# A two-layer decoder step: 32x32 tiles for the delta rule's inverse, three halving sums in the layer norm, a first weight tile loaded a phase ahead, and another order of the merged loop

## The chip, the cores and the metric

The kernel runs on one core of a Trainium2 chip, in one launch. The metric is device microseconds of the whole program, the median of several runs. One further execution was recorded by the profiler; the rows below are of that execution. TensorE is called PE (its weight loads PEld), VectorE DVE, ScalarE ACT, GpSimd POOL, and SyncE, which issues most transfers, SP. Each engine runs its own instructions in order and waits on counting semaphores.

## The reference

The program is one step of a decoder of two layers (model width 1024) for a prompt of 1024 rows and 8 sample rows together (1032 columns in the kernel's transposed layout). Cut to what matters:

```python
def even_mixer(x, ...):                    # layer 0
    qkv_a, beta_a, a_a, gate_a, q_b, kv_b, g_b = split_cols(x @ w_in, EVEN_SIZES)
    o_a, S_new = gated_delta_chunked(qa, ka, va, g, beta, S0)    # 4 heads of 128
    o_b, rows, new_buf = nsa_mixer(q_b, kv_b, gates, hist, ...)  # 8 query heads of 64, 2 groups
    return concat(rms_norm(o_a) * silu(gate_a), o_b) @ w_out

def gated_delta_chunked(...):              # for every chunk and head
    A  = where(strict, (k * beta) @ k.T * Ldec, 0)
    Tm = triangular_solve(eye + A, eye)    # the inverse, by levels in the kernel
    u, w = Tm @ (v * beta), Tm @ (k * beta * exp(gam))
    v_new = u - w @ S;  o = qg @ S + qk @ v_new;  S = S * glast + kd.T @ v_new

# nsa_mixer: three softmax branches with gates: compressed blocks of 32 rows, selected blocks of 64, window of 512
# layer 1: gated linear attention (GLA) in chunks of 16, then @ w_out
# after every mixer and every SwiGLU: x = layer_norm(ALPHA * x + f(x))
def swiglu(x, wg, wu, wd): return (silu(x @ wg) * (x @ wu)) @ wd
```

## The kernel before, in words

Matrices with weights are computed with three matmuls each (high*high, low*high, high*low parts; lines L565 to L567), with x transposed: 8 blocks of 128 features by 1032 columns, handled as NB = 3 groups of CW = 344 columns. Phases follow each other with a barrier between them: the even projection (0 to 341 us), small gates, **the merged loop** (`even_core_phase`, 377 to 1234), the sample rows of the even mixer (`sample_even_phase`, to 1337), **the chain of layer 0** (`chain_phase`: output projection, norm, SwiGLU, norm, next projection; to 2521), GLA (`gla_phase`, to 2733), and **the chain of layer 1** (to the end).

**The merged loop** interleaves three things on every engine in an order written by hand. The 1024 prompt rows are 8 tiles; `Fori i` runs 4 times, each time two chunks c (halves), each with 8 units u. A unit is one (row tile t, KV group g) of the sparse attention: `scores_win` (L1560, L1562: window and compressed scores), its maximum on DVE (`max_win`, L1925 to L1931), its exponentials on ACT (`exp_win`, L1771 to L1773), its weights on DVE (`weigh_win`, L1946 to L1950, called done by the semaphore `win_scaled`), `turn_win` (L1584: transposes of the weights on PE, in groups 0 and 1 of up to four blocks), ACT's copies of them (`keep_win`, L1784), and products with the values (`values_sel`, `values_win`); likewise `scores_sel` (L1549, always for the next unit j+1), `max_sel`, `exp_sel` (L1763), `weigh_sel`, `turn_sel` (L1572), `keep_sel`. Besides these a chunk has 24 steps `delta(c, k)` of the delta rule, three to a unit (k = 3u, 3u+1, 3u+2), and one page of the cache per unit (`pages_mean`, `pages_turn`, `pages_kept`, `pages_score`). In a chunk with many keys (t = 4 to 7) the local weights have two groups, in the others one or two.

The delta rule's inverse is built by 7 levels, `lv = (k - 3) // 2`. Before, every level works on tiles of 4 heads of 128x128: POOL masks A with a table (`masked`, L1507), PE multiplies it with D (`each`, L1639, four 128x128x128 matmuls), ACT copies the product (L1828), PE multiplies again twice, DVE subtracts from D and DT (L2008, L2010). k = 4 to 12 are the levels 0 to 4, k = 13 to 16 the levels 5 and 6. k = 3 makes A = KK and QK, two `each`, after waiting for ACT's copies VB and KE (L1820, L1823).

**The chain**: its first tile of the output projection (n = 0) waits for POOL's split of the weights into parts (`split`: L509 cast, L511 subtraction) and for h_lo (L940, DVE, 8 pieces). A norm goes by column group c: `total` (L897 additions), a matmul for the mean (L582), `centre` (L907), squares on ACT (L796), `fold` (L902: sum of 8 squares blocks by one `tensor_reduce`), a matmul for the variance, scale, low. At the end of layer 1 `turn(n)` turns each of 9 row tiles by 8 transposes (L709) and makes its row mean by 8 matmuls of one column (L715); DVE then scales the rows (L1071, L1078) for the output.

Of the kernel before, what the change touches and what calls it, by code (L numbers as in the profile page):

```python
# [47 lines left out]
LEVELS = 7  # L48


def constants():
# [4 lines left out]
    for lv in range(LEVELS):  # L56
        s = 1 << lv
        row, col = i[None, :], i[:, None]
        level[:, lv] = (row // (2 * s) == col // (2 * s)) & (row // s % 2 == 1) & (col // s % 2 == 0)
    upper = (i[:, None] <= i[None, :]).astype(np.float32)  # L60
# [8 lines left out]
    for h in range(HEADS):  # L69
# [8 lines left out]
        "c_ident": ident, "c_level": level.reshape(P, -1), "c_upper": upper, "c_causal": causal, "c_oldest": oldest,  # L78
# [289 lines left out]
class Norm:  # L368
# [3 lines left out]
    def __init__(self, nc, tag, ln, rows, low):  # L372
        self.ln, self.rows, self.low = ln, rows, low
        (self.totalled, self.mean_ready, self.centred, self.squared, self.folded, self.var_ready, self.logged,
         self.rstd_ready, self.scaled, self.rounded, self.low_ready) = [nc.alloc_semaphore(tag + s) for s in (
            "_totalled", "_mean_ready", "_centred", "_squared", "_folded", "_var_ready", "_logged", "_rstd_ready",
            "_scaled", "_rounded", "_low_ready")]


def chain_phase(nc, r, layer, tag, lay, load_out, reload, odd=None):  # L380
# [23 lines left out]
    with phase(nc) as ctx:  # L404
# [7 lines left out]
        o_hi = at("o_w_hi", [P, 3, KD, P], F32R, lay["o_hi"])  # L412
        F, Flo = at("f", [P, KF, N], F32, 0), at("f_lo", [P, KF, N], F32R, 0)
# [8 lines left out]
        sums_b = at("sums_b", [P, NB, CW], F32, KD)  # L422
        flat_f, flat_h1 = [t[:].rearrange("p k n -> p (k n)") for t in (F, H1)]
# [26 lines left out]
        def _(sp):  # L450
            def fetch_out(n):
                if n >= 3:
                    sp.wait_ge(product_o, 3 * (n - 2))
                for dst, src in load_out(n):
                    sp.dma_start(o_raw[:, n % 3][dst], src).then_inc(w_in_o[n % 3], 16)
# [26 lines left out]
            for n in range(3):  # L482
# [5 lines left out]
            for n in range(3, KD):  # L488
# [17 lines left out]
        def _(pool):  # L506
# [6 lines left out]
            def split_out(n):  # L513
                s = n % 3
                split(w_in_o[s], 16 * len(load_out(n)) * (n // 3 + 1), w_split_o, n, o_hi[:, s], o_raw[:, s], o_lo[:, s])
# [24 lines left out]
            for n in range(3):  # L540
# [3 lines left out]
            for n in range(3, KD):  # L544
# [7 lines left out]
            for n in range(2 * KD):  # L552
                split_down(n)
                if odd and n >= 13:
                    collect(evicted_d, 3 * KD, sums_b, summed_b, n - 12)
            if odd:
                for m in range(4, 6):
                    collect(evicted_d, 3 * KD, sums_b, summed_b, m)
# [2535 lines left out]
```

## Time and profile before

| | us |
|---|---|
| median of 3 runs (lowest, highest) | 3650.86 (3647.32, 3657.77) |
| the profiled execution | 3649.13 |
| its span | 3647.3 |
| PE busy in the span | 3336.8 (91%) |
| DVE busy | 1271.2 (35%) |
| POOL busy | 1016.9 (28%) |
| ACT busy | 699.8 (19%) |

The profiled execution is 1.8 us longer than its span and 1.7 us under the median. PE is busy nearly all the time in the projections and the two chains; in the merged loop, the sample rows and GLA it is not.

### The profile page before, as it was taken

How to read it: one execution, taken by the hardware profiler on the slowest of the kernel's cores; microseconds unless marked ns; L12 is line 12 of the kernel's file. 1: busy time of each engine (PE TensorE's matmuls, PEld its weight loads, DVE VectorE, ACT ScalarE, POOL GpSimd, SP SyncE). 2: the span in 40 equal slices, each digit the busy share in tenths (PEclk: the TensorE clock that was granted, in tenths of full speed). 3: DMA queues.
4: the chain of work that ended last, by engine and by line, in shares of the span. 5: the costliest groups of instructions: out<-in, count | busy, mean ns of one | idle time of the engine just before them, and what ended most of it. 6: DMA issues, size and time to landing. Idle time of an engine off the chain costs nothing. (4 is left out here: it accounts for less than half of the span.)

```text
span 3647.3 us, 55768 instructions
## 1 busy us (share of the span) xinstructions
PE 3336.8 (91%) x22086; PEld 3032.4 (83%) x22086; DVE 1271.2 (35%) x2434; ACT 699.8 (19%) x1424; POOL 1016.9 (28%) x619
## 2 busy tenths in 40 slices
PE   8998768898989769999999999998889899999998
PEld 7998546565656559999999999997659899999998
DVE  6712535555555533300004216112553500003123
ACT  1101334443444321200001102001320300001011
POOL 3542111211122024233333242331336133333220
PEclk9999889899988779999999999998779999999999
DMA  4122332323233560111111112111113011111111
GB/s 131 46 46 56 109 111 82 91 81 94 81 89 85 173 232 24 41 46 46 46 46 46 48 41 81 47 46 30 47 43 115 24 46 46 46 46 47 48 48 67
DMA packets 327512, 247.87 MB, mean 68 GB/s; under 512 B 28368, under 2 KB 322009, under 8 KB 325644
## 3 DMA queue, kind: packets, MB, share of 16 engines
q1 hardware_dynamic: 325956, 234.57, 21.8%
q10 hardware_dynamic: 720, 8.55, 0.6%
q8 instruction: 127, 2.08, 0.2%
q0 software_dynamic: 640, 2.10, 0.2%
q14 instruction: 69, 0.57, 0.1%
HBM read 220.59 MB, written 45.63 MB: 73 GB/s over the span
## 5 line engine op out<-in xcount | busy, mean ns | idle before, releaser
L565 PE MATMUL ps<-X_rounded,c_w_hi 128*128 128x344 f32 x2712 | 872.7, 322 | 6.0 <-DVE c_xla L921 5.4
L567 PE MATMUL ps<-X_rounded,c_w_rounded 128*128 128x344 f32 x2712 | 868.3, 320 | 0.0
L566 PE MATMUL ps<-c_xla,c_w_hi 128*128 128x344 f32 x2112 | 674.5, 319 | 0.0
L509 POOL CAST c_w_hi<-c_w 128x1024 fp32r<-128x1024 f32 (+1 forms) x145 | 165.4, 1141 | 1283.8 <-DMA c_w<-in_w_ffn_gate 710.2
L565 PEld LDWEIGHTS ps<-X_rounded,c_w_hi 128*128 128x128 f32 x2712 | 509.6, 188 | 8.7 <-issue 6.6
L567 PEld LDWEIGHTS ps<-X_rounded,c_w_rounded 128*128 128x128 f32 x2712 | 509.3, 188 | 0.0
L566 PEld LDWEIGHTS ps<-c_xla,c_w_hi 128*128 128x128 f32 x2112 | 398.1, 189 | 0.7 <-issue 0.2
L511 POOL TENSOR_TENSOR c_w_rounded<-c_w,c_w_hi 128x1024 fp32r<-128x1024 f32 (+1 forms) x145 | 387.1, 2670 | 11.6
L565 PE MATMUL ps<-c_f_hi,c_w_hi 128*128 128x344 f32 x1056 | 342.9, 325 | 12.6 <-DVE c_f_lo L987 12.4
L567 PE MATMUL ps<-c_f_hi,c_w_rounded 128*128 128x344 f32 x1056 | 340.8, 323 | 0.0
L566 PE MATMUL ps<-c_f_lo,c_w_hi 128*128 128x344 f32 x1056 | 339.1, 321 | 0.0
L983 DVE TENSOR_TENSOR c_f<-c_silu,ps 128x344 f32 x108 | 55.4, 513 | 763.0 <-PE ps L567 763.0
L929 DVE SCALAR_TENSOR_TENSOR X<-X,ps 128x344 f32<-128x344 f32 x144 | 72.7, 512 | 488.2 <-PE ps L567 488.2
L565 PEld LDWEIGHTS ps<-c_f_hi,c_w_hi 128*128 128x128 f32 x1056 | 200.5, 190 | 16.1 <-DVE c_f_lo L987 15.8
L295 PE MATMUL ps<-X_rounded,in_even_w_hi 128*128 128x344 f32 (+1 forms) x648 | 209.1, 323 | 4.7 <-DVEq L324 2.7
L297 PE MATMUL ps<-X_rounded,in_even_w_rounded 128*128 128x344 f32 (+1 forms) x648 | 208.3, 321 | 0.0
L296 PE MATMUL ps<-Xl_in_even,in_even_w_hi 128*128 128x344 f32 (+1 forms) x648 | 207.7, 321 | 0.0
L566 PEld LDWEIGHTS ps<-c_f_lo,c_w_hi 128*128 128x128 f32 x1056 | 200.8, 190 | 0.4 <-issue 0.2
L567 PEld LDWEIGHTS ps<-c_f_hi,c_w_rounded 128*128 128x128 f32 x1056 | 200.2, 190 | 0.0
L838 ACT ACTIVATE c_silu<-ps 128x344 f32<-128x344 f32 x108 | 49.4, 457 | 768.6 <-PE ps L567 768.6
L566 PE MATMUL ps<-c_xlb,c_w_hi 128*128 128x344 f32 x600 | 191.7, 320 | 0.0
L565 PE MATMUL ps<-c_h_hi,c_o_w_hi 128*128 128x344 f32 x384 | 128.2, 334 | 23.6 <-POOL c_o_w_lo L511 23.6
(501 smaller groups left out, 5468.6 us busy)
## 6 DMA issues: line engine op xcount, KB each, us to landing
X<-in_cache_nsa_kv SPq DMA_DIRECT2D x256, 192.0 KB, 2.4
c_w<-in_w_ffn_gate SPq DMA_DIRECT2D x44, 512.0 KB, 3.8
c_w<-in_w_ffn_up SPq DMA_DIRECT2D x44, 512.0 KB, 3.8
c_w<-in_w_ffn_down SPq DMA_DIRECT2D x32, 704.0 KB, 4.7
v_packed<-in_cache_nsa_kv SPq DMA_DIRECT2D x256, 64.0 KB, 2.5
in_even_w<-in_w_in_even SPq DMA_DIRECT2D x52, 256.0 KB, 3.1
c_w<-in_w_in_odd SPq DMA_DIRECT2D x50, 256.0 KB, 3.3
x_spilled<-H ACTq DMA_DIRECT2D x2, 4128.0 KB, 13.4
```

Of the source, the lines that this page charges most:

```text
L295: pe.matmul(dst, hi[:, u, k, 0:rows], r.Xh[:, k, cols], start=(k == 0), stop=False)
L296: pe.matmul(dst, hi[:, u, k, 0:rows], r.Xl[:, k, cols], start=False, stop=False)
L297: mm = pe.matmul(dst, lo[:, u, k, 0:rows], r.Xh[:, k, cols], start=False, stop=(k == KD - 1))
L509: pool.tensor_copy(whi, wraw).then_inc(w_split, 1)
L511: pool.tensor_tensor(wlo, wraw, whi.bitcast(F32), ALU.subtract).then_inc(w_split, 1)
L565: pe.matmul(dst, whi, xhi, start=first, stop=False)
L566: pe.matmul(dst, whi, xlo, start=False, stop=False)
L567: return pe.matmul(dst, wlo, xhi, start=False, stop=last)
L838: act.activation(lit[:, g % 2, :], r.ps[:, g % 3 * 2, 0:CW], ACT.Silu).then_inc(lit_ready, 1)
L929: v.scalar_tensor_tensor(out=dst, in0=dst, scalar=factor, in1=r.ps[:, bank, 0:CW], op0=ALU.mult, op1=ALU.add).then_inc(evicted, 1)
L983: v.tensor_tensor(flat_f[:, bass.ds(i * (2 * N) + (g // 3 * N + g % 3 * CW), CW)], lit[:, g % 2, :], r.ps[:, g % 3 * 2 + 1, 0:CW], ALU.mul ...
```

## The change

It has four parts. (1) **Chains.** The weight tile n = 0 of each output projection is loaded and split in the phase before (`sample_even_phase`, `gla_phase`): SP issues its loads there, POOL casts and subtracts. The ring of the chain starts at n = 1. (2) **Norms.** `fold` is three additions that halve (4, 2, 1 blocks of 344 columns), and `centre(na, 0)` stands ahead of `add_out(20, 6, 1)` on DVE. (3) **The end of layer 1.** POOL sums the blocks 0 to 5 (`collect`, as it does in layer 0), and `turn(n)` makes the row mean first, of 3 parts, and then the transposes. (4) **The merged loop.** The levels 0 to 4 work on the 32x32 blocks of the diagonal (`each32`: 16 matmuls of 32x32x32, in bank rows and columns of their own), with copies and updates of 128 columns in place of 512; four DVE operations cut A32 out of A, at level 4 four more each write D and DT back into full tiles that POOL has cleared. `each(6)` of k = 3 waits for VB alone. The order of the steps changes on PE and ACT.

```diff
-            pe.wait_ge(w_split_o, 2)
             for k in range(KD):
                 pe.wait_ge(h_split, k + 1)
                 for c in range(NB):
-                    mm = three(r.ps[:, c, 0:CW], o_hi[:, 0, k, :], o_lo[:, 0, k, :], h_hi[:, k, cols(c)],
+                    mm = three(r.ps[:, c, 0:CW], o0_hi[:, k, :], o0_lo[:, k, :], h_hi[:, k, cols(c)],
...
                 pe.wait_ge(evicted_d, (44, 44, 46, 46, 46, 48, 48, 48, 48)[n])
                 if n in user:
                     pe.wait_ge(row_shaped, user[n] + 1)
-                for k in range(KD):
-                    mm = pe.transpose(r.ps[0:rows, tile_bank[n] + k // 4, k % 4 * P:(k % 4 + 1) * P],
-                                      r.X[:, k, n * P:n * P + rows], r.ident[:])
-                mm.then_inc(turned, 1)
                 if n:
                     pe.wait_ge(row_centred, n)
+                pe.wait_ge(summed_b, (13, 13, 14, 14, 14, 15, 15, 15, 15)[n])
+                cut = slice(n * P, n * P + rows)
+                parts = (flat_sums[:, cut], r.X[:, 6, cut], r.X[:, 7, cut])
+                for q, part in enumerate(parts):
+                    mm = pe.matmul(r.ps[0:rows, 0, n:n + 1], part, r.ones_d[:, 0:1], start=(q == 0), stop=(q == 2))
+                mm.then_inc(row_mean, 1)
                 for k in range(KD):
-                    mm = pe.matmul(r.ps[0:rows, 0, n:n + 1], r.X[:, k, n * P:n * P + rows], r.ones_d[:, 0:1],
-                                   start=(k == 0), stop=(k == KD - 1))
-                mm.then_inc(row_mean, 1)
+                    mm = pe.transpose(r.ps[0:rows, tile_bank[n] + k // 4, k % 4 * P:(k % 4 + 1) * P], r.X[:, k, cut],
+                                      r.ident[:])
+                mm.then_inc(turned, 1)
...
+                sq = nm.rows[:, :, cols(c)]
                 v.wait_ge(nm.squared, c + 1)
-                v.tensor_reduce(sums[:, c, :], nm.rows[:, :, cols(c)].rearrange("p k n -> p n k"), AX.X,
-                                ALU.add).then_inc(nm.folded, 1)
+                v.tensor_tensor(sq[:, 0:4], sq[:, 0:4], sq[:, 4:8], ALU.add).then_inc(nm.halved, 1)
+                v.wait_ge(nm.halved, 2 * c + 1)
+                v.tensor_tensor(sq[:, 0:2], sq[:, 0:2], sq[:, 2:4], ALU.add).then_inc(nm.halved, 1)
+                v.wait_ge(nm.halved, 2 * c + 2)
+                v.tensor_tensor(sums[:, c, :], sq[:, 0], sq[:, 1], ALU.add).then_inc(nm.folded, 1)
...
             total(na, 0, 7, evicted_o, 20, 1)
+            centre(na, 0)
             add_out(20, 6, 1)
-            centre(na, 0)
             fold(na, 0)
...
             def masked(c, lv):
                 if lv >= 2:
                     pool.wait_ge(p_ready, c * LEVELS + (lv - 1))
-                pool.tensor_tensor(AM[:, lv % 2], AT[:], level[:, lv, :].unsqueeze(1).to_broadcast([P, 4, P]),
-                                   ALU.mult).then_inc(am_ready, 1)
+                if lv < SMALL_LEVELS:
...
+            def each32(b, lhs, rhs):
+                pe.sem_inc(ordered, 1)
+                for h in H4:
+                    for g in range(4):
+                        at_ = slice(32 * g, 32 * g + 32)
+                        mm = pe.matmul(bank32(b)[at_, h, :], lhs[at_, h, :], rhs[at_, h, :], start=True, stop=True)
...
+                    pe.wait_ge(vb_ready, c + 1)
+                    each(6, KTd, KTd)
                     pe.wait_ge(kdv_ready, c + 1)
                     pe.wait_ge(kbg_ready, c + 1)
-                    each(6, KTd, KTd)
                     each(7, KTd, QT).then_inc(kk_ready, 1)
                 elif k == 4:
                     pe.wait_ge(am_ready, c * LEVELS + 1)
-                    for h in H4:
-                        mm = pe.transpose(bank(6)[:, h, :], AM[:, 0, h, :], r.ident[:])
-                    mm.then_inc(p_ready, 1)
+                    each32(6, AM32[:, 0], ident32).then_inc(p_ready, 1)
...
+                        if lv < SMALL_LEVELS:
+                            each32(p_bank(lv), AM32[:, lv % 2], D32).then_inc(p_ready, 1)
+                        else:
+                            each(p_bank(lv), AM[:, lv % 2], Dm).then_inc(p_ready, 1)
                     else:
                         pe.wait_ge(p_kept, c * (LEVELS - 1) + lv)
                         pe.wait_ge(dt_updated, c * LEVELS + lv)
-                        if lv < LEVELS - 1:
-                            each(d_bank(lv), DT, PS).then_inc(d_ready, 1)
-                        each(p_bank(lv), PS, DT).then_inc(dt_ready, 1)
+                        if lv < SMALL_LEVELS:
+                            each32(d_bank(lv), DT32, PS32).then_inc(d_ready, 1)
+                            each32(p_bank(lv), PS32, DT32).then_inc(dt_ready, 1)
...
                         delta(c, 3 * u)
+                        turn_sel(i, j, 0)
                         scores_win(i, j)
-                        turn_sel(i, j, 0)
                         delta(c, 3 * u + 1)
                         turn_sel(i, j, 1)
                         pages_mean(c, u)
                         scores_sel(i, j + 1)
+                        delta(c, 3 * u + 2)
                         turn_win(i, j, 0)
                         if u % 2:
                             values_sel(i, j)
                             turn_win(i, j, 1)
-                            delta(c, 3 * u + 2)
                             pages_turn(c, u)
                             values_win(i, j)
                             pages_score(c, u)
                         else:
-                            delta(c, 3 * u + 2)
+                            pages_turn(c, u)
                             turn_win(i, j, 1)
-                            pages_turn(c, u)
...
                         exp_win(i, j)
                         delta(c, 3 * u + 1)
                         keep_sel(i, j, 1)
+                        if u % 2:
+                            delta(c, 3 * u + 2)
                         keep_win(i, j, 0)
+                        if u % 2 == 0:
+                            pages_kept(c, u)
                         exp_sel(i, j + 1)
                         keep_win(i, j, 1)
-                        delta(c, 3 * u + 2)
-                        pages_kept(c, u)
+                        if u % 2:
+                            pages_kept(c, u)
+                        else:
+                            delta(c, 3 * u + 2)
...
+                    for g in range(4):
+                        at_ = slice(32 * g, 32 * g + 32)
+                        v.tensor_tensor(A32[at_], own(bank(6), g), own(DLB, g), ALU.mult)
...
+                        if lv < SMALL_LEVELS - 1:
+                            mm = v.tensor_tensor(D32, D32, bank32(d_bank(lv)), ALU.subtract)
+                        elif lv == SMALL_LEVELS - 1:
+                            for g in range(4):
+                                at_ = slice(32 * g, 32 * g + 32)
+                                mm = v.tensor_tensor(own(Dm, g), D32[at_], bank32(d_bank(lv))[at_], ALU.subtract)
+                        else:
+                            mm = v.tensor_tensor(Dm[:], Dm[:], bank(d_bank(lv)), ALU.subtract)
...
+                if c == TT - 3:
+                    pool.wait_ge(first_in, 16 * len(first_load))
+                    pool.tensor_copy(first_hi[:], first_raw[:]).then_inc(first_split, 1)
+                    pool.wait_ge(first_split, 1)
+                    pool.tensor_tensor(first_lo[:], first_raw[:], first_hi[:].bitcast(F32), ALU.subtract)
...
+                if s == 4:
+                    for dst, src in first_load:
+                        sp.dma_start(first_raw[dst], src).then_inc(first_in, 16)
```

**PE, the even unit u = 4 of the first chunk** (k = 12, 13, 14). The piece starts behind its `scores_sel` (L1549) for the next unit; L1584 is `turn_win` group 0, L1639 `each`, L1625 `pages_turn`. Before:

```order
L1549 MATMUL ps<-H,ec_q 128x384
L1581 REGISTER_ALU
L1584 MATMUL ps<-ident,ec_pcmp 128x128
L1584 MATMUL ps<-ident,H 128x128 x3
L1639 MATMUL ps<-ec_dlb,ec_kt 128x128 x4
L1639 MATMUL ps<-ec_kt,ec_dlb 128x128 x4
L1623 REGISTER_ALU
L1625 MATMUL ps<-ident,X 128x128 x4
```

After (the same operations have the lines L1582, L1617, L1672 and L1658):

```order
L1582 MATMUL ps<-H,ec_q 128x384
L1672 MATMUL ps<-ec_dlb,ec_kt 128x128 x4
L1672 MATMUL ps<-ec_kt,ec_dlb 128x128 x4
L1614 REGISTER_ALU
L1617 MATMUL ps<-ident,ec_pcmp 128x128
L1617 MATMUL ps<-ident,H 128x128 x3
L1656 REGISTER_ALU
L1658 MATMUL ps<-ident,X 128x128 x4
```

The two `each` of k = 14 (still 128x128, a level-5 step) have moved from behind the local turn to ahead of it.

**PE, the start of the same unit.** L1560 and L1562 are `scores_win`, L1572 is `turn_sel` group 0. Before:

```order
L1639 MATMUL ps<-ec_dlb,ec_kt 128x128 x4
L1639 MATMUL ps<-ec_kt,ec_dlb 128x128 x4
L1560 MATMUL ps<-H,ec_q 128x384
L1562 MATMUL ps<-ec_kcb,ec_q 128x32
L1572 MATMUL ps<-ident,H 128x128 x3
L1680 REGISTER_ALU
L1681 REGISTER_ALU
L1639 MATMUL ps<-ec_qt,X 128x128 x4
```

After (L1593, L1595 and L1605; L1680 is `each32`, L1672 `each`):

```order
L1680 MATMUL ps<-X 32x32 x32
L1605 MATMUL ps<-ident,H 128x128 x3
L1593 MATMUL ps<-H,ec_q 128x384
L1595 MATMUL ps<-ec_kcb,ec_q 128x32
L1720 REGISTER_ALU
L1721 REGISTER_ALU
L1672 MATMUL ps<-ec_qt,X 128x128 x4
```

k = 12 is now 32 matmuls of 32x32, and the turn of the selected weights stands ahead of the window scores.

**ACT, the even unit u = 2 of the first chunk.** L1771 and L1773 are `exp_win`, L1828 the copy of delta step 7, L1784 `keep_win`, L1763 `exp_sel` of the next unit, L1797 `pages_kept`. Before:

```order
L1771 ACTIVATE ec_pcmp,ec_den<-ps,ec_ntop 128x32
L1773 ACTIVATE H,ec_den<-ps,ec_ntop 128x256
L1827 REGISTER_ALU
L1828 COPY ec_dlb<-ps 128x512
L1783 REGISTER_ALU
L1784 COPY X<-ps 128x384
L1762 REGISTER_ALU
L1763 ACTIVATE H,ec_den<-ps,ec_ntop 128x256
L1796 REGISTER_ALU
L1797 COPY X<-ps 128x512
```

After (L1817 and L1819, L1876, L1830, L1809, L1843):

```order
L1817 ACTIVATE ec_pcmp,ec_den<-ps,ec_ntop 128x32
L1819 ACTIVATE H,ec_den<-ps,ec_ntop 128x256
L1874 REGISTER_ALU
L1876 COPY X<-ps 128x128
L1829 REGISTER_ALU
L1830 COPY X<-ps 128x384
L1842 REGISTER_ALU
L1843 COPY X<-ps 128x512
L1808 REGISTER_ALU
L1809 ACTIVATE H,ec_den<-ps,ec_ntop 128x256
```

The copy of the page's keys has moved from behind `exp_sel` to ahead of it, and the copy of the delta step is a quarter as wide.

## Rows read from the trace of the kernel before

**Rows 1.** Busy time by stretch: loop, sample rows, GLA; engines, PE clock, DMA share, GB/s.

```profile
377.00:1234.00 857.00, 718.23 (x5059) 508.71 (x5059) 467.67 (x1242) 337.00 (x851) 147.58 (x120) 0.90 0.31 88
1234.00:1337.00 103.00, 65.78 (x820) 51.74 (x820) 32.07 (x97) 21.14 (x56) 7.12 (x9) 0.64 0.72 250
2521.00:2733.00 212.00, 178.38 (x1320) 125.18 (x1320) 121.82 (x240) 67.27 (x104) 65.42 (x61) 0.69 0.14 44
```

**Rows 2.** Waits of PE in the loop: us, times, longest.

```profile
PE ps L1639 <- ACT ec_kd L1823: 28.0, 8, 4.2
PE ps L1584 <- DVE ec_pcmp L1950: 27.5, 34, 2.0
...
PE ps L1584 <- DVE ec_pcmp L1955: 15.3, 8, 2.4
```

**Rows 3.** Groups of GLA on PE by line: busy us, mean ns.

```profile
L2360 PE MATMUL ps<-gl_ql,gl_en 128*32 128x16 f32 x256 | 5.7, 192 | 0.0
```

**Rows 4.** Timeline of unit 4 in the fifth chunk: start, duration (us).

```profile
878.75 0.58 ACT L1828 COPY ec_dlb<-ps 128x512 f32<-128x512 f32 x1
...
879.49 0.30 DVE L1950 TENSOR_SCALAR ec_pcmp<-ec_pcmp,ec_coef,ec_gates 128x32 f32<-128x32 f32 x1
...
879.91 0.32 PE L1584 MATMUL ps<-ident,ec_pcmp 128*128 128x128 f32 x1 [0.54 <-DVE ec_pcmp L1950]
...
880.40 1.06 PE L1639 MATMUL ps<-ec_dlb,ec_kt 128*128 128x128 f32 x8
880.60 0.58 ACT L1784 COPY X<-ps 128x512 f32<-128x512 f32 x1 [1.27 <-PE ps L1584]
...
881.08 0.59 ACT L1763 ACTIVATE H<-ps,ec_ntop 128x384 f32<-128x384 f32 x1
...
882.39 0.68 DVE L2008 TENSOR_TENSOR ec_qt<-ec_qt,ps 128x512 f32<-128x512 f32 x1
882.83 0.58 ACT L1797 COPY X<-ps 128x512 f32<-128x512 f32 x1 [1.06 <-PE ps L1625]
...
883.12 1.05 PE L1639 MATMUL ps<-ec_qt,X 128*128 128x128 f32 x7 [0.34 <-DVE ec_qt L2008]
```

**Rows 5.** Waits of PE in the chain of layer 0.

```profile
PE ps L565 <- POOL c_o_w_lo L511: 12.0, 1, 12.0
PE ps L582 <- DVE c_sums_a L902: 8.2, 3, 5.0
...
PE ps L582 <- DVE c_sums_b L902: 2.5, 1, 2.5
```

**Rows 6.** Waits of PE in the chain of layer 1.

```profile
PE ps L565 <- POOL c_o_w_lo L511: 11.7, 1, 11.7
PE ps L582 <- DVE c_sums_a L902: 8.1, 3, 5.0
```

**Rows 7.** DVE groups in the chain of layer 1: busy us, mean ns.

```profile
L902 DVE TENSOR_REDUCE c_sums_a<-c_ya 128x344 f32<-128x2752 f32 x3 | 16.0, 5317 | 4.2 <-ACT c_ya L796 4.2
...
L907 DVE TENSOR_TENSOR X<-X,ps 128x2752 f32<-128x2752 f32 x3 | 9.0, 3011 | 0.0
```

**Rows 8.** Timelines of DVE and POOL at the starts of the two chains.

```profile
1338.29 15.26 DVE L940 TENSOR_TENSOR c_h_lo<-H,c_h_hi 128x1032 fp32r<-128x1032 f32 x8 [2.65 <-ACT c_h_hi L818]
1359.65 1.38 DVE L929 SCALAR_TENSOR_TENSOR X<-X,ps 128x344 f32<-128x344 f32 x3 [6.09 <-PE ps L567]
...
1343.93 3.20 POOL L511 TENSOR_TENSOR c_o_w_lo<-c_o_w,c_o_w_hi 128x1024 fp32r<-128x1024 f32 x1
...
2734.68 16.08 DVE L940 TENSOR_TENSOR c_h_lo<-H,c_h_hi 128x1032 fp32r<-128x1032 f32 x8 [2.62 <-ACT c_h_hi L818]
2755.24 1.37 DVE L929 SCALAR_TENSOR_TENSOR X<-X,ps 128x344 f32<-128x344 f32 x3 [4.48 <-PE ps L567]
```

**Rows 9.** Timeline of PE and DVE at the end.

```profile
3628.82 1.84 PE L715 MATMUL ps<-ones_d,X 128*128 128x1 f32 x16
...
3633.40 1.28 DVE L1071 SCALAR_TENSOR_TENSOR c_y_stage<-ps,c_row_stat,c_g_row 128x1024 f32<-128x1024 f32 x1
```

More of the change, by code:

```diff
@@ L59, in constants @@
         level[:, lv] = (row // (2 * s) == col // (2 * s)) & (row // s % 2 == 1) & (col // s % 2 == 0)
+    own32 = i[:, None] // 32 * 32 + np.arange(32)[None, :]
+    small = [np.take_along_axis(level[:, lv], own32, 1) for lv in range(SMALL_LEVELS)]
+    level = np.concatenate(small + [level[:, lv] for lv in range(SMALL_LEVELS, LEVELS)]
+                           + [np.take_along_axis(ident, own32, 1)], 1)
     upper = (i[:, None] <= i[None, :]).astype(np.float32)
@@ L480, in fetch_odd @@
                     sp.dma_start(raw[:, KH * s:KH * s + KD][dst], src).then_inc(w_in_p[s], 16)
-            for n in range(3):
+            for n in range(1, 4):
                 fetch_out(n)
@@ L487, in _ @@
                 fetch_up(n)
-            for n in range(3, KD):
+            for n in range(4, KD):
                 fetch_out(n)
@@ L538, in collect @@
                     pool.tensor_tensor(sums[:, c, :], first, r.X[:, m, cols(c)], ALU.add).then_inc(summed, 1)
-            for n in range(3):
+            for n in range(1, 4):
                 split_out(n)
@@ L543, in _ @@
                 split_up(n)
-            for n in range(3, KD):
+            for n in range(4, KD):
                 split_out(n)
@@ L553, in _ @@
                 split_down(n)
-                if odd and n >= 13:
+                if n >= 13:
                     collect(evicted_d, 3 * KD, sums_b, summed_b, n - 12)
-            if odd:
-                for m in range(4, 6):
-                    collect(evicted_d, 3 * KD, sums_b, summed_b, m)
+            for m in range(4, 6):
+                collect(evicted_d, 3 * KD, sums_b, summed_b, m)
             for n in range(n_odd):
@@ L1379, in even_core_phase @@
         KT = room(2, 512)
-        level = room(LEVELS, P)
+        tables = room((SMALL_LEVELS + 1) * 32 + (LEVELS - SMALL_LEVELS) * P)
+        n32, nfull = SMALL_LEVELS * 32, (LEVELS - SMALL_LEVELS) * P
+        level32 = tables[:, 0:n32].rearrange("p (l n) -> p l n", n=32)
+        level = tables[:, n32:n32 + nfull].rearrange("p (l n) -> p l n", n=P)
+        ident32 = tables[:, n32 + nfull:n32 + nfull + 32].unsqueeze(1).to_broadcast([P, 4, 32])
+        A32, D32, DT32, PS32 = [room(4, 32) for _ in range(4)]
         upper, pool32, ng = sb("upper", [P, P]), sb("pool32", [P, 32]), sb("ng", [P, 1])
@@ L1424, in even_core_phase, with bank32, own @@
         gate_view = r.tok[:, :, R_NSA:R_NSA + 24].rearrange("p t (g h b) -> p t g h b", g=2, h=4)
[L1425 removed]
+        def bank32(b):
+            return r.ps[:, b, 0:P].rearrange("p (h n) -> p h n", h=4)
+        def own(tile, g):
+            return tile[32 * g:32 * g + 32, :, 32 * g:32 * g + 32]
         def bank(b):
@@ L1827, in delta @@
                     act.wait_ge(p_ready, c * LEVELS + (lv + 1))
-                    act.copy(PS[:], bank(p_bank(lv))).then_inc(p_kept, 1)
+                    if lv < SMALL_LEVELS:
+                        act.copy(PS32, bank32(p_bank(lv))).then_inc(p_kept, 1)
+                    else:
+                        act.copy(PS[:], bank(p_bank(lv))).then_inc(p_kept, 1)
                 elif k == 17:
```

120 lines of the change are left out of this document (83 added, 37 removed).

## The prediction, made before the changed kernel ran

> **What bounds the kernel now.** I read the busy shares by stretch first. In the projections and the two chains PE is busy for nearly all of the time, so there only waits of PE and its own instructions count. The merged loop is another matter: PE is busy for 718.2 of 857 us and the others for less than 468 [rows 1], so no engine is full; PE is the nearest to it, and 139 us of its time are waits. The list of PE's waits in that stretch names them [rows 2]: 28.0 us at step k = 3 of the delta rule, behind ACT's last copy, 8 times, so 3.5 us a chunk; and 27.5 + 15.3 = 42.8 us in which the local turns wait for `weigh_win`, 5.4 us a chunk. The rest is spread over the delta steps. The timeline of one unit [rows 4] shows why: a unit is a ring. The copy of the turned local weights on ACT (880.60) stands ahead of `exp_sel` for the next unit (881.08), after which DVE may update D (882.39), after which PE starts the next delta step (883.12). Whatever delays `exp_sel` delays the ring.
>
> In the chains the waits are few: PE waits 12.0 us and 11.7 us for the first weight tile, and 8.2, 2.5 and 8.1 us for folds [rows 5, 6].
>
> **Part 1, first weight tile.** Before, POOL subtracts the tile from 1343.93 to 1347.13, and PE begins then. The other operand, h_lo, comes from DVE in 8 pieces that end at 1353.55, and the first eviction starts at 1359.65 [rows 8]. With the tile ready, PE follows DVE piece by piece and the first group is done about a microsecond behind the last piece (an estimate), near 1354.5: 5.2 us earlier. In layer 1 h_lo ends at 2750.76 and the eviction starts at 2755.24 [rows 8]: 3.5 us earlier by the same reckoning. So the waits of 23.7 us [rows 5, 6] shrink, but only 8.7 us come back, since h_lo is late next. The price: the 0.5 MB tile is loaded in the sample phase, where transfers run at 250 GB/s with a DMA share of 0.72 [rows 1] and PE waits for them at its end: 2.1 us, bounds 0 and 2.1. In GLA the load has room (DMA share 0.14 [rows 1]), but POOL spends the cast and the subtraction, 3.2 us for the second [rows 8] and some two for the first, ahead of the last chunk's gates and states; bounds 0 and 5.3 us, I take 2.5. Net -8.7 + 2.1 + 2.5 = **-4 us**.
>
> **Part 2, folds.** A reduction over 8 blocks takes 5317 ns, an operation of 2752 elements by two operands 3011 ns, so 1.094 ns an element [rows 7]. The halving sums handle 1376 + 688 + 344 = 2408 elements: 2.63 us, and with two more starts I take 3.0; each fold ends 2.3 us earlier. `centre` ahead of the addition for block 20 is worth up to another 2 us for the first group. The first wait of 5.0 us in either layer [rows 5, 6] falls to about 0.7, the shorter ones vanish: 18.8 us of waits become 1.8, **-17 us** (bounds -19, and -9 if the ACT squares in front turn out to be late).
>
> **Part 3, the end.** Eight one-column products are 16 records in 1.84 us [rows 9]; three are 6 records, 0.69 us, 1.15 us less per turn. DVE's last stretch begins at 3633.40 [rows 9], behind six turns: 6 x 1.15 = **-7 us**, bounds -5 and -8. POOL's sums that the means now need are cheap and earlier than the last evictions.
>
> Outside the loop the sum is -4 - 17 - 7 = **-28 us**.
>
> **Part 4, the loop.** (a) Small tiles. Eight records of an `each` take 1.06 us, and the next follows 0.9 us after the first [rows 4]. For 16 matmuls of 32x32x32 the nearest row is GLA's L2360, 128*32 weights by 16 columns: 5.7 us of busy time for 256 records, 22 ns each [rows 3]. 32 records of this kind are 0.71 us; the other bound is one after another at twice that and more, 1.6 us. I take 0.65 to 0.7: 0.25 us less than before, 13 times a chunk, 3.3 us, of which five sixths (718.2 of 857) count, -2.7. (b) `each(6)` of k = 3 goes ahead of ACT's second four copies and fills 1.06 us of the 3.5 us wait, more where PE still runs at the lower clock: -2.0. (c) The moved third step fills some of the 5.4 us in which the local turns waited, in the odd units mainly: -1.5. (d) Against this stands the even unit. In the unit shown P is copied at 878.75 + 0.58 = 879.33 [rows 4]; k = 14, two wide `each` of 0.9 us, now runs from about 879.4 to 881.3, ahead of the turn, which before started at 879.91. The copy of the turned weights, 0.7 us behind the turn's start (880.60), comes at 882.0, `pages_kept` takes 0.58 more [rows 4], and `exp_sel` starts at 883.2 and not at 881.08: 2.1 us late, and with it the D update and the next delta step. The 0.4 us that k = 12 gains goes off that: +1.7. Laid out in the same way, u = 6 costs +1.5 to +3.2, since there the turn of the selected weights of u = 7, now ahead of its window scores, also waits for those late weights; u = 2, with small steps only, costs +0.65. Together +5. (e) Placing the selected turn ahead of the window scores elsewhere delays `win_scaled`: +1.2. Sum -2.7 - 2.0 - 1.5 + 5.0 + 1.2 = **0 us a chunk**, with bounds: only the gains -6.2, only the losses +6.2, so -50 and +50 us in eight chunks; the two offset each other by different mechanisms, and I take -20 to +20 as likely. DVE's shorter updates and POOL's narrower masks gain nothing by themselves, since both engines wait for most of the loop; the four A32 operations and POOL's two clearings hide in the same idle time.
>
> **A rule against it.** The row says that small tiles side by side cost 22 ns a record [rows 3]; but its tiles share all 128 rows. The Trainium skill, TensorEngine Tiling (Array Packing), Gotcha 1: PSUM Pressure, states that different row tiles cannot access the same PSUM bank simultaneously, and the four row tiles of `each32` all write one bank. By it the 32 records would go one behind another. Its price by rows is the rival below.
>
> **Rivals.**
> - *The loop gains.* The even units' hold is absorbed, because the turn was waiting anyway, and the gains stand: -4.5 us a chunk, -36 in all, 3649.13 - 28 - 36 = 3585. For it: 42.8 us of waits at exactly the place where the step is moved to. Against it: the chain shown above does not wait for the turn but for the copy behind it. 0.18.
> - *The loop loses.* The losses stand and the small tiles save nothing, since PE was waiting there: +3.8 us a chunk, +30, total 3651. That is no change. For it: five sixths is a mean, and in the short chunks the delta chain is bound by its copies and updates. 0.20.
> - *Small tiles one after another* (slower). 32 records at 0.05 us each are 1.6 us, 0.7 more than an `each`, 13 times a chunk: +9.1, +73 in all; 3649 - 28 + 73 = 3694. It decides from about 1.2 us for an `each32`. For it: the rule above, and the loop's clock of 0.90 could sink to GLA's 0.69 [rows 1], where PE works on tiny products. Against it: 22 ns a record. 0.10.
> - *The chains give half.* h_lo or the squares are late instead: -14, 3635. 0.05.
>
> **How the numbers follow.** The neutral loop has 0.47. Against the profiled execution, 3649.13, it gives 3621; that execution lies 1.7 us under the median, so in terms of the median 3623; I say 3622. Its own range is 3602 to 3643. The range for 8 in 10 takes in the gaining loop down to 3587 and the losing one up to 3655, and leaves out the serial tiles. A measurement of this kernel can tell 0.3%, 11 us: faster is then under 3640. Faster: 0.47 less a little at its upper end (0.44), 0.18, 0.05 and 0.06 of the losing loop, 0.73; same: 0.14; slower: 0.10 for the serial tiles and 0.03 for a worse losing loop, 0.13.
>
> **What would show it.** Part 1: PE's wait at the chains' first product under 3 us, then waits on h_lo, and the first evictions 5 and 3.5 us earlier relative to the chains' beginnings. Part 2: folds as three DVE operations of about 3 us together, waits on them near 2 us in all. Part 3: turns of 0.7 us products, the last DVE stretch 7 us sooner. Part 4: 32 records of `each32` within 0.8 us; the wait at k = 3 at some 1.5 us a chunk; in the even units u = 4 and 6 `exp_sel` two us later after `weigh_win`; the loop within 20 us of 857. Wrong would be: `each32` over 1.2 us, a loop clock well under 0.90, or even units that are not longer.

## The result: slower, in the merged loop alone

The changed kernel takes 3681.43 us in the median (3678.20 to 3700.71, 4 runs) against 3651.27 us (3647.32 to 3657.77, 4 runs). The ratio is 1.0092, with a 95% interval of 1.0054 to 1.0130: slower by 0.9%. Forecast were 3622 us, and at most 3655 for 8 in 10. The profiled execution has a span of 3677.9 us, 30.6 more than before.

By the first and last instruction of each phase, the time went to one place:

| phase | before, us | after, us | difference |
|---|---|---|---|
| even projection and gates | 377 | 379 | +2 |
| merged loop | 854.7 | 910.5 | +55.8 |
| sample rows | 99.1 | 101.4 | +2.3 |
| chain of layer 0 | 1183.7 | 1171.2 | -12.5 |
| GLA | 211.2 | 213.8 | +2.6 |
| chain of layer 1 | 911.9 | 891.5 | -20.4 |

The last four lines add up to -28.0 us, which is what was forecast for them. The loop was forecast at 0 and lost 56.

The busy times by stretch after, in the same form and columns as [rows 1], PE first and the granted clock of PE third from the end:

```profile
379.40:1290.00 910.60, 757.41 (x7587) 500.07 (x7587) 438.83 (x1322) 324.94 (x851) 113.56 (x136) 0.79 0.29 83
1290.00:1397.00 107.00, 65.41 (x820) 51.58 (x820) 32.08 (x97) 21.08 (x56) 10.49 (x11) 0.63 0.74 248
2569.00:2783.00 214.00, 178.55 (x1320) 126.44 (x1320) 124.31 (x240) 67.41 (x104) 69.33 (x63) 0.69 0.14 46
```

In the loop PE is now busy for 757.4 us and was for 718.2, although it has less to multiply. The clock tells why: 0.79 and not 0.90. There are two levels, 1.2 GHz (0.50) and 2.4 GHz (1.00), so a mean of 0.79 over 910.6 us is about 380 us at the lower one, and 0.90 over 857 us was about 170. PE's waits, 910.6 - 757.4 = 153 us, were 139: of the 56 us some 14 are waiting, and 39 are busy time that PE needs more at the lower clock, for less work.

PE's waits in the loop after (time, times, longest), to be held against [rows 2]:

```profile
PE ps L1672 <- DVE ec_qt L2076: 20.9, 8, 2.6
...
PE ps L1680 <- DVE X L2070: 16.9, 8, 2.1
PE ps L1672 <- ACT ec_vb L1866: 16.9, 8, 2.1
PE ps L1605 <- DVE H L1995: 15.9, 8, 2.3
PE ps L1672 <- ACT ec_kd L1870: 11.5, 8, 2.0
...
PE ps L1617 <- DVE ec_pcmp L2006: 7.5, 6, 1.7
...
PE ps L1617 <- DVE ec_pcmp L2011: 3.4, 4, 0.9
```

Of the 42.8 us in front of the local turns 7.5 + 3.4 = 10.9 are left. In their place stand three waits that come once a chunk, 2.1 to 2.6 us at their longest: for L2070, L2076 and L1995, 16.9 + 20.9 + 15.9 = 53.7 us. They lie in front of the first PE steps behind u = 2, 4 and 6, the even units. The one behind u = 0, at k = 3, has not shrunk: it is split into 16.9 us for VB and 11.5 us for KE, 28.4 together, and was 28.0.

One of them, u = 4 of the sixth chunk, in the timeline (start, duration), to be held against [rows 4] (there it is the fifth chunk, with 384 columns in `exp_sel` and not 896):

```profile
1015.62 0.58 ACT L1878 COPY ec_dlb<-ps 128x512 f32<-128x512 f32 x1
...
1016.25 1.16 PE L1672 MATMUL ps<-ec_dlb,ec_kt 128*128 128x128 f32 x8
1016.49 0.30 DVE L2006 TENSOR_SCALAR ec_pcmp<-ec_pcmp,ec_coef,ec_gates 128x32 f32<-128x32 f32 x1
...
1018.14 0.27 PE L1617 MATMUL ps<-ident,ec_pcmp 128*128 128x128 f32 x1
...
1018.78 0.59 ACT L1830 COPY X<-ps 128x512 f32<-128x512 f32 x1 [2.20 <-PE ps L1617]
1019.26 0.59 ACT L1843 COPY X<-ps 128x512 f32<-128x512 f32 x1
...
1019.74 1.02 ACT L1809 ACTIVATE H<-ps,ec_ntop 128x896 f32<-128x896 f32 x1
...
1021.75 0.68 DVE L2076 TENSOR_TENSOR ec_qt<-ec_qt,ps 128x512 f32<-128x512 f32 x1
...
1022.48 1.90 PE L1672 MATMUL ps<-ec_qt,X 128*128 128x128 f32 x8 [2.63 <-DVE ec_qt L2076]
```

k = 14 (L1672 at 1016.25) runs ahead of the local turn, which could have begun behind 1016.79 and begins at 1018.14. ACT's copy of it, then the page keys (L1843), then `exp_sel` (L1809 at 1019.74), then the update of D (1021.75), then the next step, at 1022.48: the chain that was forecast, and PE has nothing left to do but wait 2.63 us. What the forecast did not have is the next thing in that row: the eight records of the step take 1.90 us, where seven took 1.05 in [rows 4]. The clock has fallen, as the stretches of 4 us there show (columns: PE busy, PEld, DVE, ACT, POOL, granted clock, DMA share, GB/s):

```profile
1018.50:1022.50 4.00, 1.13 (x10) 0.66 (x8) 1.58 (x4) 2.34 (x5) 0.00 (x0) 1.00 0.20 61
1022.50:1026.50 4.00, 4.00 (x14) 3.02 (x15) 0.53 (x1) 1.17 (x2) 0.00 (x0) 0.57 0.47 124
1026.50:1030.50 4.00, 4.00 (x28) 2.48 (x26) 2.60 (x8) 1.52 (x5) 0.00 (x0) 1.00 0.37 94
```

Here, where steps of 128x128 follow, it is back in under 4 us. In the even unit u = 2 of the same chunk, where steps of 32x32 follow, it stays down for longer. PE waits 2.14 us until 992.11, for the update of D:

```profile
987.30 0.85 PE L1680 MATMUL ps<-X 32*32 32x32 f32 x64 [0.41 <-ACT X L1876]
...
992.11 0.65 PE L1680 MATMUL ps<-X 32*32 32x32 f32 x32 [2.14 <-DVE X L2070]
```

The stretches, in the same columns:

```profile
987.50:991.50 4.00, 2.18 (x73) 1.57 (x61) 2.64 (x7) 2.23 (x5) 0.00 (x0) 1.00 0.14 31
991.50:995.50 4.00, 3.40 (x38) 2.09 (x39) 0.66 (x3) 0.85 (x2) 1.27 (x1) 0.56 0.41 122
995.50:999.50 4.00, 4.00 (x80) 2.63 (x79) 2.04 (x8) 1.32 (x5) 0.00 (x0) 0.50 0.44 134
999.50:1003.50 4.00, 4.00 (x39) 1.82 (x39) 2.20 (x6) 0.36 (x2) 0.39 (x1) 0.50 0.04 9
1003.50:1007.50 4.00, 3.98 (x39) 3.06 (x37) 1.50 (x5) 2.33 (x5) 0.87 (x1) 0.73 0.00 0
1007.50:1011.50 4.00, 4.00 (x95) 2.56 (x94) 1.83 (x6) 0.63 (x2) 0.00 (x0) 1.00 0.31 77
```

Behind the gap the stretches of 0.56, 0.50, 0.50 and 0.73 make some 13.7 us at the lower clock, with PE busy nearly all the while: 7 us of full-speed work, so 6 to 7 us are lost behind a gap of two. The same place in the kernel with this order and 128x128 tiles (the experiment called order alone below), behind a gap of 2.45 us that ends at 1003.84:

```profile
999.50:1003.50 4.00, 1.65 (x14) 1.18 (x12) 1.50 (x4) 2.23 (x5) 0.00 (x0) 0.99 0.15 49
1003.50:1007.50 4.00, 3.66 (x14) 3.08 (x15) 0.89 (x2) 1.17 (x2) 1.27 (x1) 0.58 0.46 143
1007.50:1011.50 4.00, 4.00 (x33) 2.91 (x32) 3.05 (x9) 1.42 (x5) 0.00 (x0) 1.00 0.30 83
```

The gap is longer there and the lower clock lasts a quarter of the time. So here the order makes the gap, and the small tiles behind it make it dear.

### The profile page after: what moved, and what is told of

Its sections match the earlier page's. It is cut to its first block and busy times, and to the rows that moved or that the text cites. A ratio compares the mean times of both kernels' runs of the same rounds, so it can differ in the third digit from the quotient of the medians.

```text
span 3677.9 us, 60860 instructions
## 1 busy us (share of the span) xinstructions
PE 3364.0 (91%) x24524; PEld 3014.2 (82%) x24524; DVE 1231.2 (33%) x2528; ACT 687.5 (19%) x1424; POOL 997.1 (27%) x650
## 5 line engine op out<-in xcount | busy, mean ns | idle before, releaser
L573 PEld LDWEIGHTS ps<-X_rounded,c_w_hi 128*128 128x128 f32 x2712 | 510.9, 188 | 10.9 <-issue 9.0
L300 PEld LDWEIGHTS ps<-X_rounded,in_even_w_hi 128*128 128x128 f32 (+1 forms) x648 | 122.5, 189 | 5.6 <-DVEq L329 2.8
```

Source lines behind the costliest of these rows:

```text
L300: pe.matmul(dst, hi[:, u, k, 0:rows], r.Xh[:, k, cols], start=(k == 0), stop=False)
L573: pe.matmul(dst, whi, xhi, start=first, stop=False)
```

## The experiments

Twelve kernels, in three groups that each ran beside the kernel before on one chip. The loop's times are those of the profiled execution of each; two executions of the same loop code (before, and the first experiment) gave 854.7 and 848.1 us, so some 7 us mean little. In "small tiles alone" the split of k = 3 is kept, too; in "loop of before, filled" it is put in.

| kernel | median, us | ratio to before (95%) | loop, us | PE busy in it | clock |
|---|---|---|---|---|---|
| before | 3651.27 | | 854.7 | 718.2 | 0.90 |
| changed | 3681.43 | 1.0092 (1.0054 to 1.0130) | 910.5 | 757.4 | 0.79 |
| chains alone | 3622.24 | 0.9940 (0.9921 to 0.9960) | 848.1 | 715.5 | 0.90 |
| small tiles alone | 3627.91 | 0.9946 (0.9931 to 0.9962) | 858.9 | 726.1 | 0.82 |
| order alone | 3704.40 | 1.0169 (1.0144 to 1.0194) | 924.6 | 761.7 | 0.86 |
| changed, fillers in even units | 3622.22 | 0.9937 (0.9919 to 0.9955) | 848.9 | 728.4 | 0.90 |
| changed, even units as before | 3620.03 | 0.9911 (0.9891 to 0.9931) | 845.3 | 707.3 | 0.84 |
| changed, window scores first | 3689.91 | 1.0099 (1.0082 to 1.0116) | 922.5 | 774.2 | 0.77 |
| changed, page keys late | 3675.72 | 1.0069 (1.0042 to 1.0097) | 906.6 | 770.1 | 0.78 |
| changed, more fillers | 3603.83 | 0.9872 (0.9856 to 0.9888) | 833.6 | 732.7 | 0.95 |
| even units as before, filled | 3612.69 | 0.9875 (0.9853 to 0.9898) | 837.7 | 728.6 | 0.92 |
| changed, fillers in odd units | 3730.83 | 1.0202 (1.0179 to 1.0225) | 959.7 | 799.7 | 0.82 |
| loop of before, filled | 3603.91 | 0.9857 (0.9834 to 0.9880) | 827.7 | 738.8 | 0.96 |
| changed, PE's even units as before | 3725.61 | 1.0193 (1.0167 to 1.0219) | 950.6 | 779.6 | 0.76 |

My theory was that the order in the even units holds up `exp_sel`, that PE falls idle behind it and that its clock falls with it. The first rival: the small tiles leave PE too little work in any order. The second: the longer ring itself costs the time, at either clock.

**Which part: chains, tiles or order.** The chains alone take the changed file with the loop of before put back whole.

> The chains, folds and end as changed, the merged loop as before. If the parts outside the loop gained what the phases of the trace say (-12 in layer 0's chain, -20 in layer 1's, +2 to +3 in each of the phases that load a tile ahead), the time is 3622 to 3628 and the loop 855 us. If instead part of the 32 us gained there comes from a later start or another state, it is above 3635.

It is 3622.24 us, 24.7 less than the runs of before beside it. The gain outside the loop is real. The next two leave one half of the loop's change each:

```diff
                         delta(c, 3 * u)
-                        turn_sel(i, j, 0)
                         scores_win(i, j)
+                        turn_sel(i, j, 0)
...
                         scores_sel(i, j + 1)
-                        delta(c, 3 * u + 2)
                         turn_win(i, j, 0)
```

(and the rest of PE's and ACT's order likewise: small tiles alone), and

```diff
-SMALL_LEVELS = 5
...
-                        each32(p_bank(lv), AM32[:, lv % 2], D32).then_inc(p_ready, 1)
+                        each(p_bank(lv), AM[:, lv % 2], Dm).then_inc(p_ready, 1)
```

(all levels 128x128, k = 3 as before, the order as changed: order alone).

> The changed kernel with the order of before on PE and ACT, the small tiles kept. Theory O (the order delays exp_sel in even units, PE falls idle there and its clock falls): the loop is back at 825 to 860 us with a clock of 0.88 or more, the time 3595 to 3628. Theory T (small tiles leave PE too little work, whatever the order): the loop stays above 885 us with a clock under 0.84, the time 3650 or more.

> The order of the changed kernel on PE and ACT with the 128x128 tiles of before and k = 3 as before. Theory O: the loop is well over 855 us, 880 to 910, time 3645 to 3680, with idle of two to three us before the next delta step in even units. Theory T: the loop is 845 to 865 us, the time 3612 to 3632.

The order alone costs 924.6 - 848.1 = 76 us, more than the whole change. Its waits are those of the even units, 40.3 us for the update of D alone (us, times, longest):

```profile
PE ps L1648 <- DVE ec_qt L2022: 40.3, 16, 2.6
```

The small tiles in the old order are no gain: 858.9 us and thus 11 more, within the lines that I drew for the first theory but not inside its clock, 0.82 and not 0.88. PE's waits are as long as without them, 858.9 - 726.1 = 132.8 us and 848.1 - 715.5 = 132.6; it is PE's busy time that rises, from 715.5 to 726.1, with less to do. So the first rival holds in part. By the mean clocks of the table, worked out as above, PE is at the lower level for about 170 us in the chains alone, 310 with the small tiles, 260 with the order and 380 with both (estimates): the fall of the clock has two sources, and the tiles are the larger one. In the changed order the small tiles and the split of k = 3 together take 14 us off (924.6 to 910.5).

**Clock or ring.** Behind the last local turn of each even unit stand eight 128x128x128 matmuls into a corner of the window scores' bank that nothing reads:

```diff
                             pages_turn(c, u)
                             turn_win(i, j, 1)
+                            for q in range(8):
+                                pe.matmul(s_win[:, 800:928], r.ident[:], causal[:], start=True, stop=True)
```

> The changed kernel with eight matmuls of 128x128x128 that nothing reads behind the last local turn of every even unit, 32 x 8, some 58 us of extra PE work at the higher clock. Theory C (most of the lost time is what the clock costs behind idle gaps of two to three us): gaps are filled, the loop's clock rises from 0.79 to 0.86 or more, and the loop falls by 10 to 35 us in spite of the work. Theory H (the ring itself is longer, at either clock): the loop stays at 910 or grows by up to 30 us.

The loop falls by 62 us. The row of the whole loop, in the columns of [rows 1]:

```profile
378.29:1227.18 848.89, 728.42 (x8099) 504.92 (x8099) 438.45 (x1322) 324.45 (x851) 114.34 (x136) 0.90 0.31 89
```

256 matmuls are added and PE is busy for 29 us less. This is the clock; the second rival, a longer ring at either clock, had the loop stay or grow. A control puts the same matmuls into the odd units, where no gap of the changed kernel lies:

```diff
                         if u % 2:
+                            for q in range(8):
+                                pe.matmul(s_win[:, 800:928], r.ident[:], causal[:], start=True, stop=True)
                             values_sel(i, j)
                             turn_win(i, j, 1)
```

> Control: the same eight matmuls as in the filler kernel, but in the odd units, behind the first local turn, where the changed kernel shows no gap. Theory C: nothing of the loss comes back, the loop is 910 to 965. If more PE work keeps the clock up wherever it stands, the loop falls to 870 or less as it did with the fillers in even units.

```profile
PE ps L1672 <- DVE ec_qt L2078: 20.9, 8, 2.6
...
PE ps L1680 <- DVE X L2072: 16.9, 8, 2.1
```

These two waits (us, times, longest) are those of the changed kernel to a tenth, and the loop is 49 us longer: nothing of the loss comes back, and most of the added work is paid. What helps is not more work but work in the gap.

**Which move in the even units.** PE's and ACT's parts were undone together, each alone, and the third move, the selected turn ahead of the window scores, by itself:

```diff
-                        delta(c, 3 * u + 2)
+                        if u % 2:
+                            delta(c, 3 * u + 2)
                         turn_win(i, j, 0)
...
                         else:
-                            pages_turn(c, u)
+                            delta(c, 3 * u + 2)
                             turn_win(i, j, 1)
+                            pages_turn(c, u)
```

(PE; with ACT's order in even units as before as well: even units as before) and

```diff
-                        if u % 2 == 0:
-                            pages_kept(c, u)
                         exp_sel(i, j + 1)
+                        if u % 2 == 0:
+                            pages_kept(c, u)
```

(ACT alone: page keys late).

> The changed kernel with the even units as before (the third delta step on PE behind the local turn, the page keys on ACT behind exp_sel), the odd units and the selected turn ahead of the window scores as changed. If the even units' hold and the idle behind it are most of the loss: loop 855 to 875 us, time 3620 to 3645. If the odd units or the order of turn and scores are: loop over 890.

> The changed kernel with the page keys on ACT behind exp_sel in even units, all else as changed. The copy of 0.58 us comes off the hold in 32 units: 19 us by itself, and more where the gap then no longer lowers the clock: loop 870 to 892. If ACT's place of that copy does not matter, the loop stays at 905 to 915.

> The changed kernel with only PE's part of the even units undone (third delta step behind the local turn), ACT's order as changed. With ACT's part alone undone the loop fell by 4 us, with both by 65. If PE's step is the cause: loop 845 to 860. If the two only work together: 885 or more.

Both undone: 845.3, a fall of 65 us. ACT's alone: 906.6, where 870 to 892 were expected; that fall of 4 is no more than two runs of one loop differ. PE's alone: 950.6, slower than the change by 40. So neither is the cause by itself: with PE's step ahead of the turn, `exp_sel` stands behind the copy of a late turn; with PE's step put back but the page keys still ahead of `exp_sel` on ACT, `exp_sel` (L1811 here) waits behind the page keys (L1845) for the page's turn (L1658), which PE does behind its step:

```profile
1050.49 0.59 ACT L1845 COPY X<-ps 128x512 f32<-128x512 f32 x1 [1.85 <-PE ps L1658]
1050.97 1.01 ACT L1811 ACTIVATE H<-ps,ec_ntop 128x896 f32<-128x896 f32 x1
```

The last expectation was wrong in the direction, since I had read the two as adding up. Even units as before, in the columns of [rows 1]:

```profile
379.56:1224.85 845.29, 707.32 (x7587) 473.28 (x7587) 439.38 (x1322) 326.22 (x851) 114.88 (x136) 0.84 0.31 89
```

The instructions on PE are those of the changed kernel, 7587 records, and take 707.3 us and not 757.4: 50 of the 65 us are the clock and 15 are waiting.

> The changed kernel with the window scores ahead of the selected turn again, all else as changed. By the term given to that move (1.2 us a chunk) the loop falls by about 10 us, from 910 to 900. If the turn's wait for late weights holds the window scores and is what makes the ring long, it falls by 25 us or more.

Also wrong: the loop did not fall by 10 us or more. In the profiled execution it is 12 us longer, 922.5, but that execution is 8 us above the median of its kernel, and the ratios to before, 1.0099 and 1.0092, have intervals that overlap. So no cost of the turn ahead of the scores shows, and no gain either.

**A better version.** With more fillers in the changed kernel (the first product of k = 3 done three times, six matmuls ahead of k = 4, eight ahead of the last local turn of a chunk), and in the two other loops (the diff leaves out that the wait for `kept` moves ahead of the last fillers):

```diff
                     each(6, KTd, KTd)
+                    each(6, KTd, KTd)
+                    each(6, KTd, KTd)
...
+                    warm(s_sel[:, 0:P], 6)
                     pe.wait_ge(am_ready, c * LEVELS + 1)
...
+                if j % HALF == HALF - 1 and n == 0:
+                    warm(r.ps[:, 4, 0:P], 8)
                 pe.wait_ge(win_scaled, i * NU + (j + 1))
```

> The kernel with fillers in even units, with more of the same: each(6) of k = 3 done three times, six matmuls ahead of k = 4's wait, eight ahead of the last local turn's wait. Theory C (the lower clock behind gaps is what is lost): the loop's clock rises from 0.90 to 0.95 or more and the loop falls from 849 to 805 to 835. If the work costs as much as it saves: 845 to 860.

> The even units as before with small tiles, plus matmuls that nothing reads in its remaining gaps (ahead of the local turn in units 0, 2, 4 and 7, at k = 3 and k = 4). Theory C: the loop's clock rises from 0.84 to 0.93 or more and the loop falls from 845 to 800 to 828, time 3575 to 3603, the best so far. If gaps cost only their own length, the loop stays at 840 to 855.

> The merged loop of before with its 128x128 tiles and order (the chains as changed), with k = 3 split and its first product done three times, and matmuls that nothing reads ahead of k = 4 and ahead of the local turn in units 0, 1 and 7. Theory C: loop 815 to 835 with a clock of 0.94 or more, from 848 and 0.90. If the lower clock costs little in that loop: 845 to 860.

```profile
379.31:1212.94 833.63, 732.72 (x8451) 523.21 (x8451) 438.16 (x1322) 324.19 (x851) 113.95 (x136) 0.95 0.32 91
```

```profile
378.56:1206.23 827.67, 738.79 (x5603) 540.61 (x5603) 464.89 (x1242) 337.22 (x851) 146.39 (x120) 0.96 0.32 91
```

The first row is the changed order with more fillers, the second the loop of before, filled. The clocks are 0.95 and 0.96, the medians 3603.83 and 3603.91 us: 1.3 and 1.4% under the kernel before, with work that does nothing. The third, even units as before with the local turn filled in units 0, 2, 4 and 7, fell less than expected (837.7); its clock is 0.92, and waits of up to 3.8 us for an update of D are left, 12.4 us in all. As far as kernels with different fillers can be compared, neither the order nor the tiles matter much at a high clock: 833.6, 837.7 and 827.7. In the loop of before, filled, what the split of k = 3 gave and what the fillers gave is not separated.

## Why the prediction was wrong

**Parts 1 to 3, outside the loop: right in the sum, -28 forecast and -28.0 measured, to the last us by luck.** By the terms of the forecast about -15 us fall to the chain of layer 0 and -18 to that of layer 1; measured are -12.5 and -20.4. The waits in the two chains after, in the columns of [rows 5] and [rows 6]; first layer 0:

```profile
PE ps L573 <- DVE c_h_lo L953: 4.4, 1, 4.4
...
PE ps L582 <- DVE c_sums_b L906: 3.6, 1, 3.6
PE ps L590 <- DVE c_sums_a L916: 0.7, 1, 0.7
```

and layer 1:

```profile
PE ps L573 <- DVE c_h_lo L953: 7.4, 4, 5.1
...
PE ps L590 <- DVE c_sums_a L916: 0.7, 1, 0.7
```

The first tile is no longer waited for; h_lo is, as said, with 4.4 and 7.4 us where 12.0 and 11.7 stood, 11.9 us less where 8.7 were forecast. The first evictions are not 5.2 and 3.5 us earlier:

```profile
1399.04 13.14 DVE L953 TENSOR_TENSOR c_h_lo<-H,c_h_hi 128x1032 fp32r<-128x1032 f32 x8 [2.66 <-ACT c_h_hi L827]
1418.44 1.78 DVE L942 SCALAR_TENSOR_TENSOR X<-X,ps 128x344 f32<-128x344 f32 x4 [6.27 <-DMA X<-x_spilled]
...
2785.52 16.15 DVE L953 TENSOR_TENSOR c_h_lo<-H,c_h_hi 128x1032 fp32r<-128x1032 f32 x8 [2.55 <-ACT c_h_hi L827]
2803.75 1.36 DVE L942 SCALAR_TENSOR_TENSOR X<-X,ps 128x344 f32<-128x344 f32 x3 [2.08 <-DMA X<-x_spilled]
```

They start 19.4 and 18.2 us behind the first piece of h_lo, where [rows 8] had 21.4 and 20.6, so 2.0 and 2.3 us earlier; the trace now has them wait for a transfer of X, which the forecast did not have. The folds' waits on the first norm are 0.7 us per layer (forecast 0.7, from 8.2 and 8.1); in layer 0 PE waits 3.6 us at the second norm for the sum behind its mean (L906), which was not forecast either. The three sums, DVE in layer 1 (busy, mean ns):

```profile
L912 DVE TENSOR_TENSOR c_ya<-c_ya 128x1376 f32<-128x1376 f32 x3 | 4.8, 1589 | 3.8 <-ACT c_ya L805 3.8
...
L914 DVE TENSOR_TENSOR c_ya<-c_ya 128x688 f32<-128x688 f32 x3 | 2.6, 874 | 0.1
L916 DVE TENSOR_TENSOR c_sums_a<-c_ya 128x344 f32<-128x344 f32 x3 | 1.6, 519 | 0.1
```

1589 + 874 + 519 ns are 2.98 us; I had 3.0. The prices of the early tile are 2.3 us in the sample rows (2.1 forecast) and 2.6 in GLA (2.5). The sum is confirmed by the chains alone, -24.7 us in the median. Of Part 3 the price is confirmed, 0.72 us for the six records of a row mean (forecast 0.69):

```profile
3662.49 0.28 PE L721 MATMUL ps<-ones_d,c_sums_b 128*128 128x1 f32 x2
3662.63 0.58 PE L721 MATMUL ps<-ones_d,X 128*128 128x1 f32 x4
```

What it gave by itself no run separates. The trace of before has seven turns ahead of 3633.40 and not six, so that the reckoning of the forecast gives -8.

**Part 4a, small tiles: they are cheaper than forecast, and still no gain.** All 3328 records take 51.9 us of busy time, 0.50 us for the 32 records that were taken as 0.65 to 0.7 (group by line: busy time, mean ns, idle before):

```profile
L1680 PE MATMUL ps<-X 32*32 32x32 f32 x3328 | 51.9, 215 | 27.4 <-DVE X L2070 16.9 <-POOL X L1534 6.2 <-ACT X L1876 4.3
```

In the timeline above, at the higher clock, 64 records take 0.85 us: the four row tiles that write one bank do not go one behind another at the price of that rival (1.6 us for 32). The Trainium skill, TensorEngine Tiling (Array Packing), Gotcha 1: PSUM Pressure, has it that row tiles cannot access one bank simultaneously; no trace here shows a cost of it. But what they saved went to the clock and not to waits, as the small tiles alone showed: PE's waits stayed at 133 us, the clock fell to 0.82, and the loop grew by 11 us where 4a and 4b together had -4.7 us a chunk, -38.

**Part 4d, the even units, is the step that failed: the mechanism was right, the price was not.** `exp_sel` is late nearly as worked out: it starts 2.95 us behind the end of the local weights (1016.79 to 1019.74), where [rows 4] had 1.29, so 1.7 us later (forecast 2.1). The idle behind it was in the forecast as length alone, +5 us a chunk, +40, and the clock stood at nothing. By experiment the even units' order costs 65 us, of which only 15 are waiting and 50 are the lower clock behind the gaps. The same term, the clock, is missing in 4a. I had it only in the rival of the serial tiles, as a consequence of tiny products. That half of the rival came true (0.82 with the small tiles in the old order); its price of 1.6 us for 32 records did not. That idle gaps take PE to 1.2 GHz was to be asked of the 0.90 in [rows 1], which already was some 170 us at the lower clock.

**Parts 4b, 4c: in the changed order nothing is left of them.** The waits that 4c was to fill fell from 42.8 to 10.9 us and came back as the 53.7 us in the even units. The wait at k = 3 is 28.4 us in two pieces in the changed order, since the hold of u = 0 falls on it too; with the even units as before it is 5.9 + 10.4 = 16.3 us, against a forecast of 12. With the small tiles, the split and the odd units' order, but the even units as before, the loop is only 3 us under that of before (845.3 and 848.1), which is within what two runs differ, where the forecast without 4d had -5.0 us a chunk, -40. Its clock is 0.84. **Part 4e did not show**: +1.2 us a chunk was forecast for the turn ahead of the scores, and undoing it gave no gain (ratios 1.0099 and 1.0092).

The rival "the loop loses" had the right place at 30 us, half the size, since it too priced idle time by its length. Two sums of the rivals do not come out of the terms as they stand: the gains without 4d are -5.0 us a chunk and not -4.5, and the losses without 4a are +2.7 and not +3.8.

## What to carry to other kernels

Where a stage leaves PE idle for two us at a time, price the gap twice: by its length, and by what PE does next at half its clock. An edit that moves PE work out of such a gap can cost several times the idle time that it adds (here 65 us for 15), and one that makes the work smaller can lose to the clock all that it saves; the granted clock in short stretches of the trace of before shows which gaps are near it. Of two orders on two engines, undo both before either: each alone may hold the same ring.

## What the runs showed of the hardware that was not expected

Gaps of 2.1 to 2.6 us were enough to take PE from 1.00 to 0.50, and how long it stayed there went with what PE did next. By the granted clock of the traces the changed kernel is at the lower level for 10 to 14 us behind each of the eight gaps at u = 2, where steps of 32x32 follow, though PE is busy nearly all the while, and for under 4 us behind each of the eight at u = 4, where steps of 128x128 follow. With the order alone, 128x128 throughout, it is 3 to 7 us behind u = 2, and behind five of the eight gaps of 2.6 us at u = 4 the clock does not fall at all. Behind the gaps of 2.3 us at u = 6 it is 10 us in both kernels, without steps of 32x32, so the tiles are not all of it. The Trainium skill, TensorE: Matmul & The Clock Gate, HAM oscillation — how this bites in real kernels, describes a like pattern, a wait between bursts after which the next burst starts at the lower clock, with waits for transfers of some 3 to 5 us. This case's rows agree with the pattern, in 4 us stretches of 0.56, 0.50, 0.50 and 0.73, but here waits of 2.1 us between engines did it. 256 matmuls that nothing reads made a loop of 910 us 62 us shorter, and the loop of before, untouched by the change's order and tiles, was 20 us shorter with fillers and the split of k = 3. And 16 matmuls of 32x32x32 on the diagonal cost 0.4 to 0.5 us, about half of four of 128x128x128 (which follow each other at 0.9).
